# Convolution taps of a YOCO-style trunk: one transfer of 31 rows, or two of 16

## What is computed

```
h = rmsnorm(x, a_norm)
a, b, z = split(h @ a_w_in)                     # 2048 -> 3 * 2048
u = a * sigmoid(b)
c = depthwise_causal_conv(u, a_conv_w) + a_conv_b   # 31 taps per channel
y = silu(layernorm(c, a_ln_g, a_ln_b)) * silu(z)
x = x + y @ a_w_out
kv = rmsnorm(x, kv_norm) @ w_kv                 # keys and values of 3 dilation groups
... attention in 3 groups on rmsnorm(x, b_norm) @ b_w_in, gate, @ b_w_out, residual
out = rmsnorm(x, final_norm)
```

## Time and profile before

| | |
|---|---|
| median of 3 runs | 1543.01 us (1542.29 to 1544.58) |
| span of the profiled execution, first to last instruction | 1539.5 us |
| PE busy | 1481.3 us (96%) |
| DVE busy | 861.2 us (56%) |
| ACT busy | 704.7 us (46%) |
| POOL busy | 386.7 us (25%) |
| moved by DMA | 268.31 MB, mean 174 GB/s |

### The profile page before, as it was taken

The page is one execution under the profiler, slowest core; times in us unless marked ns, Lnnn a source line. Parts: engine busy times, 40 slices in busy tenths (PEclk is TensorE's granted clock), DMA queues, the critical chain, the costliest instruction groups (busy, mean ns, idle before and its releaser), DMA issues.

```text
span 1539.5 us, 23155 instructions
## 1 busy us (share of the span) xinstructions
PE 1481.3 (96%) x8198; PEld 1279.0 (83%) x8198; DVE 861.2 (56%) x1433; ACT 704.7 (46%) x1036; POOL 386.7 (25%) x168
## 2 busy tenths in 40 slices
PE   4999999969989999999999999999999999999997
PEld 3888888857868888888888888888888888888786
DVE  2599889873075554545555555455554554554322
ACT  5444444445464444444444444444444444444543
POOL 3888888707800000000000000000000000000595
PEclk9999999979999999999999999999999999999999
DMA  5766666604569666666566665665665656653652
GB/s 179 199 183 188 191 185 181 209 28 142 186 167 269 184 167 174 181 173 184 163 175 178 181 179 159 181 180 161 190 178 168 183 159 191 174 163 119 246 192 82
DMA packets 454095, 268.31 MB, mean 174 GB/s; under 512 B 4322, under 2 KB 436450, under 8 KB 453395
## 3 DMA queue, kind: packets, MB, share of 16 engines
q1 hardware_dynamic: 454066, 267.99, 60.7%
q10 hardware_dynamic: 6, 0.02, 0.0%
HBM read 263.70 MB, written 4.29 MB: 174 GB/s over the span
## 4 chain that ended last, share of the span: by engine, by line
issue 77%; POOL 15%; PE 5%; DMA 1%; ACT 1%; POOLq 0%; DVE 0%; SPq 0%; ACTq 0%
POOL w_lo L260 15%; PE bank L294 2%; PE bank L296 2%; PE bank L295 2%; DMA param_rows<-a_ln_b_dram 1%; ACT act_a L458 0%; ACT w_hi L251 0%; PE bank L1008 0%; POOLq L259 0%; PE bank L999 0%; ACT bank L646 0%; DVE y L964 0%; POOLq L423 0%; DVE resid L948 0%; PE bank L1099 0%
## 5 line engine op out<-in xcount | busy, mean ns | idle before, releaser
L274 PE MATMUL bank<-act_a,w_hi 128*128 128x512 f32 x2304 | 819.1, 397 | 6.2 <-DVE k_t L862 3.0
L260 POOL TENSOR_TENSOR w_lo<-raw,w_hi 128x1024 fp32r<-128x1024 f32 x160 | 385.7, 2431 | 1136.3 <-ACT w_hi L251 1136.2
L276 PE MATMUL bank<-act_a,w_lo 128*128 128x256 f32 x2304 | 649.7, 282 | 0.0
L251 ACT ACTIVATE w_hi<-raw 128x1024 fp32r<-128x1024 f32 x480 | 502.0, 1058 | 308.0 <-PE bank L276 223.1
L260 DVE TENSOR_TENSOR w_lo<-raw,w_hi 128x1024 fp32r<-128x1024 f32 x320 | 391.4, 1229 | 283.5 <-ACT w_hi L251 280.3
L274 PEld LDWEIGHTS bank<-act_a,w_hi 128*128 128x128 f32 x2304 | 433.0, 188 | 111.2 <-DVE k_t L862 3.4
L276 PEld LDWEIGHTS bank<-act_a,w_lo 128*128 128x128 f32 x2304 | 432.9, 188 | 0.0
L274 PE MATMUL bank<-act_b,w_hi 128*128 128x512 f32 x1024 | 364.3, 397 | 0.0
L276 PE MATMUL bank<-act_b,w_lo 128*128 128x256 f32 x1024 | 288.7, 282 | 0.0
L274 PEld LDWEIGHTS bank<-act_b,w_hi 128*128 128x128 f32 x1024 | 192.5, 188 | 45.9
L276 PEld LDWEIGHTS bank<-act_b,w_lo 128*128 128x128 f32 x1024 | 192.4, 188 | 0.0
(11 more groups left out here) (119 smaller groups left out, 717.1 us busy)
## 6 DMA issues: line engine op xcount, KB each, us to landing
raw<-w_kv_dram SPq DMA_DIRECT2D x96, 1024.0 KB, 6.0
raw<-b_w_in_dram SPq DMA_DIRECT2D x64, 1024.0 KB, 6.4
raw<-a_w_in_dram SPq DMA_DIRECT2D x48, 1024.0 KB, 5.8
raw<-a_w_out_dram SPq DMA_DIRECT2D x16, 1024.0 KB, 5.0
raw<-b_w_out_dram SPq DMA_DIRECT2D x16, 1024.0 KB, 5.1
bias<-bias_dram SPq DMA_DIRECT2D x16, 384.0 KB, 7.7
x_sb<-x_dram SPq DMA_DIRECT2D x2, 1024.0 KB, 6.3
resid_dram<-x_sb SPq DMA_DIRECT2D x1, 2048.0 KB, 7.7
```

Of the source, the lines that this page charges most:

```text
L251: nc.scalar.activation(w_hi[:, stream.half_slot(half), :], raw[:, slot, part:part + HALF], ACT.Copy).then_inc(hi_done, 1)
L260: eng.tensor_tensor(w_lo[:, stream.half_slot(half), :], raw[:, slot, part:part + HALF], w_hi[:, stream.half_slot(half), :].bitcast(F32), A ...
L274: nc.tensor.matmul(dst[:, 0:2 * S], w_hi[:, slot, k * P:(k + 1) * P], source[:, kt, :, :], start=(kt == 0), stop=False)
L276: mm = nc.tensor.matmul(dst[:, 0:S], w_lo[:, slot, k * P:(k + 1) * P], source[:, kt, 0, :], start=False, stop=(kt == KT - 1))
```

## The change

The taps come as two transfers of 16 rows: taps 0 to 15 into rows 0 to 15 of `param_rows`, taps 15 to 30 into rows 16 to 31. Tap 15 is fetched twice and stands in rows 15 and 16; `tap_row` finds the column of each tap. `param_rows`, `param` and `taps` become one row or column larger (38 rows, 38 columns, 33 columns), the vectors' rows move by one, and the wait counts eight transfers. SP issues five of them and ACT three, as before.

```diff
-ROW_CONV_B, ROW_LN_G, ROW_LN_B, ROW_A_NORM, ROW_KV_NORM, ROW_B_NORM = range(TAPS, TAPS + 6)
-ROWS = TAPS + 6
+TAP_ROWS = 32
+ROW_CONV_B, ROW_LN_G, ROW_LN_B, ROW_A_NORM, ROW_KV_NORM, ROW_B_NORM = range(TAP_ROWS, TAP_ROWS + 6)
+ROWS = TAP_ROWS + 6
+
+def tap_row(k):
+    return k if k < TAP_ROWS // 2 else k + 1
...
-        taps = sb("taps", [P, TAPS + 1])
+        taps = sb("taps", [P, TAP_ROWS + 1])
...
-        param_sources = ((0, a_conv_w[0]), (ROW_CONV_B, a_conv_b), (ROW_LN_G, a_ln_g), (ROW_LN_B, a_ln_b),
+        half_taps = TAP_ROWS // 2
+        param_sources = ((0, a_conv_w[0, 0:half_taps, :]), (half_taps, a_conv_w[0, half_taps - 1:TAPS, :]),
+                         (ROW_CONV_B, a_conv_b), (ROW_LN_G, a_ln_g), (ROW_LN_B, a_ln_b),
...
-            for first, src in param_sources[:4]:
+            for first, src in param_sources[:5]:
                 sp.dma_start(param_rows[first:first + src.shape[0], :], src).then_inc(rows_in, 16)
...
-            for first, src in param_sources[4:]:
+            for first, src in param_sources[5:]:
                 act.dma_start(param_rows[first:first + src.shape[0], :], src).then_inc(rows_in, 16)
...
-                                                   in0=u[:, k:k + S], scalar=taps[:, k:k + 1], in1=acc,
+                                                   in0=u[:, k:k + S], scalar=taps[:, tap_row(k):tap_row(k) + 1], in1=acc,
...
-            pe.wait_ge(rows_in, 7 * 16)
+            pe.wait_ge(rows_in, 8 * 16)
```

More of the change, by code:

```diff
@@ L713, in tap @@
                 if k == 0:
-                    nc.vector.tensor_scalar(acc, u[:, k:k + S], taps[:, k:k + 1], taps[:, TAPS:TAPS + 1],
+                    nc.vector.tensor_scalar(acc, u[:, k:k + S], taps[:, k:k + 1], taps[:, ROW_CONV_B:ROW_CONV_B + 1],
                                             ALU.mult, ALU.add).then_inc(tap_done, 1)
@@ L759, in _ @@
                 gate_out(c - 1, gate[:, bass.ds(tile_before, 1), :].rearrange("p a s -> p (a s)"))
-                load_taps(c - 1, param[:, bass.ds(tile_before, 1), 0:TAPS + 1].rearrange("p a r -> p (a r)"))
+                load_taps(c - 1, param[:, bass.ds(tile_before, 1), 0:TAP_ROWS + 1].rearrange("p a r -> p (a r)"))
                 for k in range(16):
@@ L773, in _ @@
             last = KT - 1
-            load_taps(last, param[:, last, 0:TAPS + 1])
+            load_taps(last, param[:, last, 0:TAP_ROWS + 1])
             for k in range(TAPS):
```

## The result

The changed kernel takes 1515.43 us (1514.33 to 1517.13) against 1543.71 us for the kernel before on the same chip: a ratio of 0.9819, interval 0.9805 to 0.9832, or 28 us less. The forecast was 9.8 us less and 1531.0 to 1537.0 us. The time is outside the range. The sign was right and the size was not.

What follows compares the result with a forecast made beforehand. PE was taken to bound the kernel from the first product on, after a start held by rows on one DMA engine. -9.9 + 0.1 = -9.8 us gave 1543.0 - 9.8 = 1533.2 us; 8-in-10 range 1531.0 to 1537.0.

Steps and rivals of the forecast that it cites:

- the first part: Whole kernel: PE, busy 1481.3 of 1539.5 us, sets the pace from the first product on, at 29.20 us.
- everything behind it by a microsecond: From the first product on: each microsecond taken off before it moves all later work by a microsecond.
- Slower: the new places in SBUF: PE's products: moving data 96 bytes higher could slow them, 1556.2 us at 10 ns each; chance 0.02.
- the tap's 474 to 492 ns at 31 starts: DVE's tap reads u at starts 4 bytes apart; cited as nearest evidence on new places for PE.
- The rival's own count: PE's products: 9.8 us over 2304 products with act_a is 4.3 ns of their 397, where the change loses.
- The prediction's last line: Profile after: if PE's start and first product are right but the time is not 1533, look at L274's mean.
- fewer rows in series: Parameter load at the start: 29 fewer packets on one DMA engine, 9.9 us gained, bounds 9.0 to 9.9.
- The chain behind the landing: Start, vector landing to first product: 8.74 us of PE and DVE work left alone, product at 19.3 us.
- slab 0 off the path: Start: slab 0 lands at 13.5 us, needed by 15.2, 1.7 us of room, so it does not gate.
- the gain not given back in the loops: Loops: rival that the gain is given back later, needing another pace than PE's; chance 0.01.
- The signs that hang on the landing: Start: slab 1 issue ends near 10.4, transposes begin 10.6, ACT's split about 13.6, first product 19.3 us.

Runs made afterwards that it cites:

- e10: Changed kernel, parameters issued ahead of x, plus two unused 16-row transfers behind x into neighbouring partitions 0 to 15 and 16 to 31; 1517.29 us, one execution.
- e11: Changed kernel, parameters issued ahead of x, plus two unused 16-row transfers behind x into every eighth partition; 1512.56 us, one execution.
- e2: Changed kernel with taps declared last and 64 unused bytes ahead of act_a, restoring the old SBUF places; 1538.47 us, ratio 0.9959.
- e7: Kernel before with 96 unused bytes ahead of act_a and 160 behind it, act_b 256 bytes higher; 1526.62 us, ratio 0.9879.
- e15: Changed kernel, parameters issued ahead of x, with 96 more unused bytes ahead of act_a; 1519.89 us, ratio 0.9841.
- e1: Kernel before with 96 unused bytes ahead of act_a, taps still one transfer of 31 rows; 1522.82 us, ratio 0.9856.
- e9: Changed kernel with SP's five parameter transfers issued ahead of x in place of behind it; 1513.46 us, ratio 0.9817.
- e13: Kernel before with 96 unused bytes ahead of w_hi, so weights and moving data shift together; 1545.37 us, ratio 1.0011.
- e17: Kernel before with 160 unused bytes ahead of w_hi and 96 more ahead of act_a; 1522.29 us, ratio 0.9866.

## Why the prediction was wrong, step by step

**The step that failed** is the assumption in the first part, that only the start moves and "everything behind it by a microsecond", with PE's pace left as it was. The pace was considered, in the rival "Slower: the new places in SBUF", with 0.02, in one direction, and by the wrong test: the tap's 474 to 492 ns at 31 starts speak of DVE, and its answer was carried over to PE. The rival's own count shows how sensitive the kernel is: it named 4.3 ns a product as the point that cancels 9.8 us. It counted too few products, though: `act_a`'s 2304 alone, without `act_b`'s 1024 and without the 128x256 partner of each. The products did change, by 2 to 4 ns, downwards; that is some 6 ns a pair over 3328 pairs, 20 us, and it brought the 15.0 + 4.8 us that the range left out. An equal case with the other sign, at that price, would have stood at 1533.2 - 20 = 1513 us. No row of the trace before could give the price or the sign, so what was within reach was a wider range, not the number. The shift by 96 bytes was known and named; I asked only whether it could hurt. The prediction's last line does point the right way: with the start as forecast and another time, look at L274's mean. It was said to stay 397 ns and was 394.

**The term of the sum that was mis-sized** is "fewer rows in series", taken as 9.9 with 9.0 to 9.9 as bounds. The 16 rows were spread over all engines, as taken: that step was right (16 packets of 8 KB under way at once, and the rows no longer take ten microseconds). But the price per packet was taken from packets that ran one at a time. Written by 16 engines at once beside the tail of `x`, they jammed, and `x` with them; the vector landed at 13.16 in place of 10.4, and the term is 20.32 - 13.16 = 7.2 us. That the neighbouring partitions have a share in this, e10 and e11 show; how the rest divides between the load and the rows stays open.

**What held.** The chain behind the landing (8.82 us, forecast 8.74 and at most 0.08 for the extra column); slab 0 off the path (ACT's split at 16.25, needed by 19.97 - 2.01); the gain not given back in the loops. The signs that hang on the landing came 2.3 to 2.8 us later than named: SP's issue of slab 1 ends at 12.7 us (named: 10.4), PE's transposes begin at 13.3 (10.6), ACT's split at 16.25 (13.6), the first product at 22.1 (19.3). e2 is the case that the prediction described: the transfers at the old places give 0.9959, 6.3 us less, or 1536.7 us from the 1543.0 of the forecast. That lies inside the range, at its upper edge.

**What stays open.** Why a turn costs what it costs at each distance: no run shows what the weights' and the data's reads share. Three readings show that something besides the distance modulo 256 has a small say, and it was not separated: e2's convolution loop took 277.9 us against 279.2 before at the same distance; e7's `act_b` was faster than the kernel before at the same distance; and e15 was slow in the convolution loop (279.6) and in between in the heads. Open too is the part of the jam that spreading does not remove.

## What to carry to other kernels

A change in a tensor's size moves everything declared behind it. On a kernel that PE bounds, compare the addresses of moving data and weights before and after. As a control before crediting the edit, run the old kernel with the new places (e1) and the new kernel with the old ones (e2). Row transfers into a handful of partitions: give them a count that spreads over the engines, and try them at the head of the queue. Issued first, they let the first product start 2.3 us earlier still (e9), although `x` then lands later. A packet price read from packets that ran one at a time can be far too low for many at once: 0.31 us here, and 0.9 to 1.2 under load.

## What the runs showed of the hardware that was not expected

A product of 128x512 with its 128x256 partner starts every 353 ns at a distance of 64 between the starts of its weights and of its moving data in SBUF modulo 256 bytes, and every 347 ns at a distance of 160. The timelines near 1000 us, where the second row is three pairs behind the first, give (1000.87 - 999.81) / 3 before and (1000.87 - 999.83) / 3 after:

```profile
999.81 0.40 PE L274 MATMUL bank<-act_a,w_hi 128*128 128x512 f32 x1
...
1000.87 0.40 PE L274 MATMUL bank<-act_a,w_hi 128*128 128x512 f32 x1
```

```profile
999.83 0.39 PE L280 MATMUL bank<-act_a,w_hi 128*128 128x512 f32 x1
...
1000.87 0.39 PE L280 MATMUL bank<-act_a,w_hi 128*128 128x512 f32 x1
```

Over the kernel that is some 22 us of 1545, for 96 unused bytes (e1). The Trainium skill ("SBUF — State Buffer", section "Who interferes with whom") gives PE two independent read ports, one for weights and one for moving data; by that rule the distance should not matter, and e13 against e1 and e17 shows that it does.

One transfer of 31 rows of 8 KB ran on one DMA engine at 26 GB/s, and of the two transfers of 16 rows 16 packets were under way at once. Those packets took 0.9 to 1.2 us each under load, against 0.31 when one engine worked alone.
